# The compressed branch's long contraction: blocks stationary, weights moving, result turned afterwards

## What is computed

```python
def compress(kv, pos, w1, w2):          # kv: (B, 2 groups, 512, 96)
    B, G, S, dh = kv.shape
    chunks = kv.reshape(B, G, S // CMP_STRIDE, CMP_STRIDE, dh)            # stride 16
    blocks = jnp.concatenate([chunks[:, :, :-1], chunks[:, :, 1:]], axis=3)
    flat = (blocks + pos).reshape(B, G, S // CMP_STRIDE - 1, CMP_BLOCK * dh)
    return jax.nn.gelu(flat @ w1) @ w2
...
k_cmp = compress(heads(kc), cmp_pos_k, cmp_k_w1, cmp_k_w2)
v_cmp = compress(heads(vc), cmp_pos_v, cmp_v_w1, cmp_v_w2)
```

## Time and profile before

| | |
|---|---|
| time before, median of 3 runs | 3630.57 us (3628.75 to 3630.7) |
| the profiled execution, its own time | 3629.97 us |
| its span from the first to the last instruction | 3628.2 us |
| mean granted TensorE clock | 0.979 |
| TensorE busy with matmuls | 3544.8 us (98%) |
| VectorE / ScalarE busy | 1464.8 us (40%) / 1194.2 us (33%) |
| GpSimd busy | 54.3 us (1%) |
| DMA, mean | 90 GB/s |

### The profile page before, as it was taken

The page is one execution under the profiler, slowest core; times in us unless marked ns, Lnnn a source line. Parts: engine busy times, 40 slices in busy tenths (PEclk is TensorE's granted clock), DMA queues, the critical chain, the costliest instruction groups (busy, mean ns, idle before and its releaser), DMA issues.

```text
span 3628.2 us, 39774 instructions
## 1 busy us (share of the span) xinstructions
PE 3544.8 (98%) x17601; PEld 2981.9 (82%) x17601; DVE 1464.8 (40%) x1604; ACT 1194.2 (33%) x1755; POOL 54.3 (1%) x66
## 2 busy tenths in 40 slices
PE   8999999999999999999999899999999999899999
PEld 7778788888888888888888778888888888788887
DVE  4444433337644323322344454223422354553233
ACT  3344332236534222322233343222322332432222
POOL 2000000000000000000000000000000000000000
PEclk9999999999999999999998799999999998899999
DMA  5214132223341322232223102322332222013321
GB/s 158 93 47 146 52 116 93 105 76 99 105 140 61 108 93 97 87 119 93 94 80 104 47 12 93 105 93 93 105 102 96 93 78 83 24 36 121 99 93 58
DMA packets 246333, 326.44 MB, mean 90 GB/s; under 512 B 18320, under 2 KB 215232, under 8 KB 246160
## 3 DMA queue, kind: packets, MB, share of 16 engines
q1 hardware_dynamic: 241232, 308.77, 26.3%
q0 software_dynamic: 4928, 15.12, 1.2%
HBM read 321.74 MB, written 2.10 MB: 89 GB/s over the span
## 4 chain that ended last, share of the span: by engine, by line
PE 91%; DVE 5%; ACT 4%; DMA 0%; issue 0%; POOL 0%; DVEq 0%; ACTq 0%; POOLq 0%
PE P L483 27%; PE P L484 27%; PE P L485 27%; PE P L488 3%; PE P L631 3%; PE P L609 3%; DVE WR L1429 1%; ACT WR L954 1%; DVE BIG L1437 1%; ACT BIG L961 1%; DVE BIG L1446 1%; DVE HT L1437 1%; ACT XN L961 0%; PE P L868 0%; ACT BC L961 0%
## 5 line engine op out<-in xcount | busy, mean ns | idle before, releaser
L1429 DVE TENSOR_TENSOR WR<-STG,WR 128x2048 fp32r<-128x2048 f32 (+2 forms) x300 | 669.5, 2232 | 1382.1 <-ACT WR L954 1381.8
L483 PE MATMUL P<-HT,WR 128*128 128x512 f32 (+1 forms) x3016 | 1126.4, 373 | 5.5 <-DVE WR L1429 3.0
L484 PE MATMUL P<-HT,WR 128*128 128x512 f32 (+1 forms) x3016 | 1122.9, 372 | 0.0
L485 PE MATMUL P<-HT,WR 128*128 128x512 f32 (+1 forms) x3016 | 1122.6, 372 | 0.0
L954 ACT CAST WR<-STG 128x2048 fp32r<-128x2048 f32 (+2 forms) x300 | 557.5, 1859 | 1102.1 <-PE P L485 1101.9
L483 PEld LDWEIGHTS P<-HT,WR 128*128 128x128 f32 x3016 | 571.3, 189 | 105.2 <-DVE WR L1429 3.8
L485 PEld LDWEIGHTS P<-HT,WR 128*128 128x128 f32 x3016 | 570.9, 189 | 98.4
L484 PEld LDWEIGHTS P<-HT,WR 128*128 128x128 f32 x3016 | 571.2, 189 | 97.4
L483 PE MATMUL P<-WR,HT 128*128 128x512 f32 (+1 forms) x1344 | 524.6, 390 | 12.3 <-DVE HT L1437 12.3
L485 PE MATMUL P<-WR,HT 128*128 128x512 f32 (+1 forms) x1344 | 521.6, 388 | 0.0
L484 PE MATMUL P<-WR,HT 128*128 128x512 f32 (+1 forms) x1344 | 521.3, 388 | 0.0
(11 more groups left out here) (177 smaller groups left out, 2522.8 us busy)
## 6 DMA issues: line engine op xcount, KB each, us to landing
STG<-in_w_ffn_gu_dram SPq DMA_DIRECT2D x44, 1024.0 KB, 5.0
STG<-in_ffn_w_gate_dram SPq DMA_DIRECT2D x44, 1024.0 KB, 5.3
STG<-in_ffn_w_up_dram SPq DMA_DIRECT2D x44, 1024.0 KB, 5.3
STG<-in_ffn_w_down_dram SPq DMA_DIRECT2D x44, 1024.0 KB, 4.9
STG<-in_w_ffn_down_dram SPq DMA_DIRECT2D x22, 1024.0 KB, 4.8
STG<-in_w_xkv_dram SPq DMA_DIRECT2D x16, 1024.0 KB, 5.4
STG<-in_w_in_dram SPq DMA_DIRECT2D x12, 1024.0 KB, 5.2
STG<-in_w_xq_dram SPq DMA_DIRECT2D x8, 1024.0 KB, 5.2
```

What stands on the lines that cost most here:

```text
L483: pe.matmul(o, lh, rh, start=first, stop=False)
L484: pe.matmul(o, lh, rl, start=False, stop=False)
L485: return pe.matmul(o, ll, rh, start=False, stop=last)
L1429: v.tensor_tensor(WR[0:p, n % NWR, 1, cut], STG[0:p, n % NSTG, cut], WR[0:p, n % NWR, 0, cut].bitcast(F32), ALU.subtract).then_inc(ve.sem, ...
```

## The change

The operands of the long contraction are exchanged: the blocks (62 columns) are stationary and the weights (96 columns) move, so the result comes out as 62 by 96. Both operands are now addressed over 128 rows instead of 96; rows 96 to 127 of the blocks are set to zero once per layer by GpSimd (rows 96 to 127 of `WR` keep what was there, and are multiplied by zero). ScalarE's GELU writes the 62 by 96 result into `BC` (`N_GT`); a new TensorE step `hidden_turn(z)` transposes it, and a new VectorE step `hidden(z)` copies the 96 by 62 result into `N_GH`. `second(z)` now waits for VectorE instead of ScalarE. `hidden_turn(0)` stands between heads q 4 and q 5, `hidden_turn(1)` after head k 0, and `second(1)` moves from behind head k 0 to behind head k 1.

```diff
-        N_BR = RB[0:96, 0:3968].rearrange("p (s j m) -> p s j m", s=2, j=32)
+        N_BR = RB[:, 0:3968].rearrange("p (s j m) -> p s j m", s=2, j=32)
+        N_GT = [BC[0:62, 0, 96 * z:96 * z + 96] for z in range(2)]
...
+                        g.wait_ge(*mm.at(before, "group", 2))
+                        po.memset(RB[96:128, 0:3968].bitcast(F32), 0.0).then_inc(pw_zero.sem, pw_zero.up("block_zeros", s))
...
-                return [WR[0:units[n][2], n % NWR, z, 0:k * w].rearrange("p (k n) -> p k n", k=k) for z in range(2)]
+                return [WR[:, n % NWR, z, 0:k * w].rearrange("p (k n) -> p k n", k=k) for z in range(2)]
...
                 def compress(z):
+                    g.wait_ge(*pw_zero.at("block_zeros", s))
...
-                            last = mm3(P[0:96, b, 0:62], w[0][:, j, :], w[1][:, j, :], N_BR[:, 0, jj], N_BR[:, 1, jj],
+                            last = mm3(P[0:62, b, 0:96], N_BR[:, 0, jj], N_BR[:, 1, jj], w[0][:, j, :], w[1][:, j, :],
                                        jj == 0, jj == 31)
...
+                def hidden_turn(z):
+                    b = where[s, "ght", z] = pick(ALL, (ve, (s, "gh", z)))
+                    g.wait_ge(*ac.at(s, "gh", z))
+                    tr(P[0:96, b, 0:62], N_GT[z], 62).then_inc(mm.sem, mm.up(s, "ght", z))
+
                 def second(z):
-                    g.wait_ge(*ac.at(s, "gh", z))
+                    g.wait_ge(*ve.at(s, "gh", z))
...
                 compress(0)
-                for j in range(2):
-                    head("q", 2, j, "q", ac)
+                head("q", 2, 0, "q", ac)
+                hidden_turn(0)
+                head("q", 2, 1, "q", ac)
                 drop((s, "q", 2))
                 second(0)
...
                 compress(1)
                 head("k", 0, 0, "k", ve)
-                second(1)
+                hidden_turn(1)
                 head("k", 0, 1, "k", ve)
                 drop((s, "k", 0))
+                second(1)
...
                 def gelu(z):
+                    g.wait_ge(*ve.at(prev, "x", 3))
                     g.wait_ge(*mm.at(s, "cmp", z, 16))
-                    if z:
-                        g.wait_ge(*mm.at(s, "second", 0))
-                    fn(N_GH, P[0:96, where[s, "cmp", z], 0:62], ACT.Gelu_apprx_tanh, s, "gh", z)
+                    fn(N_GT[z], P[0:62, where[s, "cmp", z], 0:96], ACT.Gelu_apprx_tanh, s, "gh", z)
...
+                def hidden(z):
+                    g.wait_ge(*mm.at(s, "ght", z))
+                    if z:
+                        g.wait_ge(*mm.at(s, "second", 0))
+                    cp(N_GH, P[0:96, where[s, "ght", z], 0:62], s, "gh", z)
...
                 blocks(1)
+                hidden(0)
...
                 key(0)
-                second(1)
+                hidden(1)
                 key(1)
+                second(1)
```

More of the change, by code:

```diff
@@ L1917, in nsa @@
                 key(0)
+                hidden(1)
+                key(1)
                 second(1)
-                key(1)
                 after((s, "k", 0))
```

## The result

The changed kernel took 3600.64 us in the median of 4 runs (3597.91 to 3603.28) against 3630.6 for the kernel before (3628.75 to 3630.7, 4 runs). The ratio is 0.9919, with a 95% interval of 0.9901 to 0.9936.

A forecast was written before the change was run, and what follows sets the result against it. TensorE, 91% of the chain, was taken as the bound. Two layers' stretches 23.9 us shorter, less 3.2 for clock dips, gave 20.7 off 3629.97; with 0.6 for the median 3609.8, given as 3609.5, range 3604 to 3618.

The forecast's parts named there:

- TensorE as the bound: Whole kernel: 91% of the chain is TensorE, so shortening its own work shortens the kernel unless it then waits.
- Pitch 0.056: Compression: each matmul loading 62 columns and moving 96 takes 0.056 us, set by loaded columns; stage of 5.4 us.
- the clock stays up through the stage: Compression: moving 96 columns per 0.056 us is dense enough to keep TensorE's clock at 1.00.
- The first stretch: From `compress(0)` to `compress(1)`, with the new stage and waits: 28.9 us in each layer.
- a wait before `second(0)`: TensorE waits about 1.0 us there for `hidden(0)`, which stands behind VectorE's queue.
- The second: From `compress(1)` to `v`: 25.0 us, plus 1.6 to 1.7 for a half-clock dip, in each layer.
- the idle time before `second(1)`: After head k 1, TensorE stands still 2.4 us until VectorE's `hidden(1)` copy is handed over.
- Sum for both layers: `compress(0)` to `v`: 23.9 us less, minus 3.2 for one half-clock dip a layer, gives 20.7 us.
- the pitch that stays at 0.084: Rival in the compression: every load with its matmul costs the same, stage 8.1 us, total near 3619; chance 0.14.
- the fall within the stage: Rival in the compression: the clock falls all the same, costing 2.5 to 3 us a stage, total near 3611; chance 0.14.
- the slower one: Rival in the compression: moving costs four cycles a column, stage 15.4 us, 17 us slower, total 3647; chance 0.03.
- the last one of the sum: Whole kernel: 20.7 us off the profiled 3629.97 gives 3609.3; the runs' median stands 0.6 higher, so 3609.8.

The follow-up runs named there:

- a3: Changed kernel, but 96 columns of the blocks' buffer loaded as stationary instead of 62, with 96 still moving; 3610.12 us, ratio 0.9954.
- b1: Kernel before with only both operands of the long contraction over 128 rows (zeros in the blocks), operands not exchanged; 3629.8 us, ratio 0.9995.
- The filler: Added 512-column matmuls with overwritten results ahead of `v`: changed kernel with 5, 3609.99 us, with 15, 3606.94; kernel before with 5 and 9, 3629.34.
- b3_copy: Kernel before, unedited, run and profiled again; 3625.9 us.
- b0_copy: Kernel before, unedited, run and profiled again; 3631.73 us.
- a1b_copy: Changed kernel, unedited, run again beside another version on the same chip; median 3604.0 us, ratio 0.9932.
- a4: Changed kernel with VectorE's copy `hidden(0)` moved before the block remainder and `hidden(1)` between the halves of the pooling; 3603.8 us, ratio 0.9924.

## Why the prediction was wrong

*Point by point.* TensorE as the bound held. "Pitch 0.056" was measured at 0.056, and the load went by columns. That the clock stays up through the stage held in all profiles with 96 moving columns. The first stretch was forecast at 28.9 us and took 28.7, with a wait before `second(0)` below the forecast 1.0. The second was forecast at 25.0 plus 1.6 for the fall and took 26.65; the idle time before `second(1)` was 2.06 of the forecast 2.4, released by VectorE's copy, with the fall right behind it. Sum for both layers: forecast 20.7, measured 20.9. Of the rivals, the pitch that stays at 0.084 appears only when 96 columns are loaded (a3; its stretches of 30.9 and 29.3 us are what that rival's sum says), the fall within the stage only when 62 move (b1), and the slower one not at all: a pitch of 0.056 us leaves at most 1.4 cycles to each of the 96 moving columns, and no run shows four. One term was mis-sized with little effect on the sum: the wait before `second(0)` was 0.2 to 0.3 us, since head q 5 ended later and the copy came earlier than forecast.

*The step that failed* is the last one of the sum, "Against the profiled execution 3629.97 - 20.7": it let everything outside the edited stretch keep its time, a term of nothing for which no reason was given, and the range carried only the falls at `second(1)` and the rivals of the stage. Two things lay outside.

First, 4.4 and 2.2 us came in the two parts behind `v`, 6.6 in all. In four profiles of the kernel before they took 980 and 571.3 to 571.5 us. In the profile after they took 975.7 and 569.2; in the two copies of the changed kernel 977.9 and 978.0, then 568.9 and 568.8, with an edited stretch 1.6 us shorter, so that the whole from `compress(0)` to the end is the same to 0.3 us in all three. The changed kernel moved `v` against the falls of the clock, and the attention behind it lost less. The 17 profiles have 34 such parts. The 16 short ones (975.5 to 975.8 and 568.8 to 569.2) are those whose first fall came 24.0 to 24.8 us behind `v`, with 17 to 20.5 us at half clock in the 85 us behind it; the other 18 had it earlier or later and 27 to 51 us at half clock. The filler shows that it is the placing and not the changed compression: 5 matmuls take 4.8 of the 6.6 us away, 15 leave them, and in the kernel before 5 and 9 bring them, in one profile each. What is only argued is the inner step, which small wait of the attention decides at each placing. No such gain was forecast, and that the placing was a good one is luck: nobody chose it.

Second, the profile after had the short part ahead (1933 us) and the profile of before a long one. Both kernels show both: of the profiles with the old compression one of 6 had the short one, of those with the new one 5 of 11, and that difference may be chance. Like with like, b3_copy (3625.9 us, part ahead 1933.19) against the profile after (3598.48, 1933.45) is 27.4 us, which is 20.9 and 6.6 less 0.1; b0_copy (3631.73, 1938.98) against the profiled copy a1b_copy (3604.51, 1939.17) is 27.2. So 27 of the 30 between the medians are accounted for. The remaining 3 fit a different mixture of short and long parts ahead in the unprofiled runs, which is not shown.

Two statements of the Trainium skill, page "TensorE: Matmul & The Clock Gate", were at stake. By section "LDWEIGHTS (loading the stationary operand)" the load goes by columns and rows do not matter; the runs agree, 0.056 us for 62 columns and 0.085 for 96, over 96 as over 128 rows. Section "Back-to-back issue gap" gives 81 ns as sustained spacing at 128 moving columns with a load each; at 96 moving and 62 loaded columns this case measured 56, so that figure is no floor for pairs that load fewer columns.

## What to carry to other kernels

Where every matmul loads its own stationary operand, try the side with fewer columns as the stationary one and let the wider one move: here the load set the pitch (0.056 us for 62 columns, 0.085 for 96), and moving 96 columns instead of 62 also kept the clock, which was worth as much as the pitch. A stage that makes TensorE wait behind another engine's queue costs the wait and often a stretch at half clock behind it: 12 of the 14 waits of 2.0 to 2.1 us at `second(1)` in these profiles were followed by 3.4 us at half, two by none. Where the clock falls in a later part of a kernel that has many short waits, an edit ahead of it can change that part's time by several microseconds in either direction, so cut two profiles at the same instructions before crediting the edit, and widen the range by what copies of the same kernel show.

## What the runs showed that was not expected

- The changed kernel, unedited, spread from 3598.05 to 3612.66 us, at mean granted clocks of 0.990 down to 0.985. The part ahead of the first compression took 1933 to 1934 or 1937 to 1939 us with identical matmuls.
- The part behind the second layer's `v` took 568.8 to 577.3 us, and the part behind the first layer's 975.5 to 983.6. The shortest and the longest lie close together in the place of the first fall: 568.8 at 24.0 us behind `v`, 577.25 at 23.9; 975.5 at 24.2, 983.60 at 23.6.
- Removing 2.06 us of idle time and the fall behind it in each layer (a4) moved the median by nothing; adding 3 matmuls of 0.23 us a layer to that took some 6 to 8 us away.
